# A quarter of the expert rows of the later prompt columns added by GpSimd to a sum of its own

## What is computed

```python
g = jax.nn.softmax(cv, axis=-1)
act = jax.nn.gelu(jnp.einsum('td,thkd->thk', xb, peer_u[e]).astype(jnp.float32))
return jnp.einsum('thk,thkd->td', (g * act).astype(xb.dtype), peer_v[e])
...
return x1 + peer_ffn(h, w_peer_q, peer_sub_keys, peer_u, peer_v).reshape(x1.shape)
```

## Time and profile before

| | |
|---|---|
| runs | 2168.15, 2169.51, 2175.05 us; median 2169.51 |
| profiled execution | 2170.43 us, of which the span (first to last instruction) 2168.6 |
| busy: PE, PEld | 1698.0 us (78%), 1236.0 us (57%) |
| busy: DVE, ACT, POOL | 1602.5 us (74%), 1257.1 us (58%), 635.5 us (29%) |
| HBM read | 690.14 MB |
| granted TensorE clock, mean | 0.835 |

### The profile page before, as it was taken

The page is one execution under the profiler, slowest core; times in us unless marked ns, Lnnn a source line. Parts: engine busy times, 40 slices in busy tenths (PEclk is TensorE's granted clock), DMA queues, the critical chain, the costliest instruction groups (busy, mean ns, idle before and its releaser), DMA issues.

```text
span 2168.6 us, 27262 instructions
## 1 busy us (share of the span) xinstructions
PE 1698.0 (78%) x8774; PEld 1236.0 (57%) x8774; DVE 1602.5 (74%) x3603; ACT 1257.1 (58%) x2751; POOL 635.5 (29%) x657
## 2 busy tenths in 40 slices
PE   7997699776896985996977987975887796765766
PEld 3554565635664654674655765654655665564554
DVE  2455676486699899869896796886898889768444
ACT  1223434226467654667897697874555465446665
POOL 1000000034334344333333333333333433333431
PEclk9998589886898886997998997987896897876666
DMA  7000300179999999999999999996999999999997
GB/s 277 20 17 13 88 1 30 49 284 420 417 414 390 419 418 390 419 379 384 419 419 374 406 400 371 419 411 248 412 368 362 405 370 385 316 417 358 420 420 302
DMA packets 108351, 695.68 MB, mean 321 GB/s; under 512 B 16688, under 2 KB 19120, under 8 KB 31408
## 3 DMA queue, kind: packets, MB, share of 16 engines
q0 software_dynamic: 95376, 674.29, 77.3%
q1 hardware_dynamic: 12832, 19.65, 3.0%
HBM read 690.14 MB, written 3.76 MB: 320 GB/s over the span
## 4 chain that ended last, share of the span: by engine, by line
PE 33%; DVE 30%; DMA 13%; ACT 10%; DVEq 4%; issue 4%; ACTq 3%; POOL 1%; POOLq 0%
DMA region<-in_peer_rows,region 12%; DVE region L1707 11%; DVE xall L1715 6%; PE ps L2244 5%; PE ps L2049 5%; DVEq L1112 4%; ACTq L1096 3%; ACT region L1100 3%; PE ps L1731 3%; PE ps L1996 2%; PE ps L2066 2%; ACT region L1097 1%; DVE region L1443 1%; PE ps L1899 1%; ACT region L1019 1%
## 5 line engine op out<-in xcount | busy, mean ns | idle before, releaser
L693 POOL DMA_INDIRECT region<-in_peer_rows,region x576 | 569.5, 989 | 1404.1 <-PE ps L2244 712.3
L1707 DVE SCALAR_TENSOR_TENSOR region<-region,h_now 128x1024 f32<-128x1024 f32 x576 | 695.7, 1216 | 208.5 <-DMA region<-in_peer_rows,region 191.8
L2244 PE MATMUL ps<-ident,region 128*128 128x128 f32 x3352 | 567.6, 327 | 253.9 <-ACT region L1100 231.8
L2244 PEld LDWEIGHTS ps<-ident,region 128*128 128x128 f32 x3352 | 472.6, 170 | 358.9 <-ACT region L1100 303.0
L1100 ACT ACTIVATE region<-region 128x1024 f32<-128x1024 f32 x419 | 481.3, 1149 | 35.5 <-issue 1.6
L1095 ACT ACTIVATE region<-region 128x1 f32<-128x1 f32 x576 | 114.5, 199 | 353.1 <-DVE region L1707 348.6
L2049 PE MATMUL ps<-w_uk_s,region 128*128 128x512 f32 x544 | 279.8, 640 | 7.1 <-ACT region L960 6.9
L1715 DVE SCALAR_TENSOR_TENSOR xall<-region,xall 128x1024 f32<-128x1024 f32 x157 | 201.8, 1285 | 68.3 <-ACT region L1097 53.3
L1097 ACT ACTIVATE region<-region 128x1 f32<-128x1 f32 x576 | 169.8, 295 | 40.7 <-issue 1.4
L2049 PEld LDWEIGHTS ps<-w_uk_s,region 128*128 128x128 f32 x544 | 100.2, 205 | 82.6 <-issue 73.9
L960 ACT ACTIVATE region<-ps 128x512 f32<-128x512 f32 x136 | 79.5, 585 | 68.7 <-PE ps L2049 66.0
(11 more groups left out here) (393 smaller groups left out, 2577.3 us busy)
## 6 DMA issues: line engine op xcount, KB each, us to landing
region<-in_w_peer_q POOLq DMA_DIRECT2D x16, 1024.0 KB
region<-in_peer_rows,region POOLq DMA_INDIRECT x576
region<-in_w_in POOLq DMA_DIRECT2D x8, 882.0 KB, 14.1
region<-in_w_peer_q SPq DMA_DIRECT2D x8, 512.0 KB, 4.3
region<-in_x_turned SPq DMA_DIRECT2D x5, 512.0 KB, 3.6
region<-in_w_out SPq DMA_DIRECT2D x2, 1024.0 KB, 12.4
region<-in_w_out SPq DMA_DIRECT2D x1, 2048.0 KB, 18.3
out_p_y<-xall SPq DMA_DIRECT2D x4, 512.0 KB
```

The lines of the kernel that those rows point to most:

```text
L693: pool.indirect_dma_start(ring[r][:], None, a["peer_rows"], bass.IndirectOffsetOnAxis(ap=experts[:, t, n:n + 1], axis=0)).then_inc(landed[ ...
L1707: v.scalar_tensor_tensor(ring[r][:, 0:D], ring[r][:, 0:D], 1.0, h_now[:], ALU.mult, ALU.mult, accum_out=acts[:, t % 2, n:n + 1]).then_inc( ...
L2244: last = te.matmul(ps[6 + c // 4][:, (c % 4) * P:(c % 4 + 1) * P], ring[r][:, D + c * P:D + (c + 1) * P], ident[:], is_transpose=True, sta ...
```

## The change

78 rows of the prompt, those with m >= 176, m % 128 >= 12 and m % 4 = 3, get a third way. ScalarE scales them as it does TensorE's (L1100). GpSimd then adds the scaled slot to `pool_acc`, which is `xall[:, 0, :]`, 128 x 1024 in f32, free once tile 0's y is stored. In GpSimd's queue the add stands just ahead of whatever is fetched into the same slot. VectorE adds `pool_acc` to `xall[:, t, :]` once a tile: at column 262 for tile 1, 390 for tile 2, and in `y_add(3)`; after the first two it clears `pool_acc` again, and the first time at column 174, after a wait for the store of y of tile 0. TensorE's `y_turn(1)` gets a wait for `sel_kept` of 2. `pool_rows`, `dve_rows` and `on_pe` replace the counts that assumed two ways.

Of the 78 rows, 63 were TensorE's and 15 VectorE's: 367, 375, 379, 399, 407, 415, 419, 427, 435, 439, 447, 455, 459, 467, 475.

```diff
--- before.py
+++ after.py
@@ -180,6 +180,7 @@
         HBUF_SLOT = len(ring)
         ring.append(Region(HBUF_AT, SIZE).view(W))
         NRING = len(ring)
+        pool_acc = xall[:, 0, :]
         h_rows = [hbuf] + [tables[:, 0:D]] * (NTILE - 1)
         late = Region(KEPT_END, OT_AT)
         I_ROW_AT = late.at
@@ -298,7 +299,7 @@
             "sk_in", "sk_turned", "skT_ready", "w_out_in", "g_ffn_in", "w_q0_in0", "w_q0_in1", "w_q0_in2", "w_used",
             "scored", "biased", "exped", "p_turned", "pT_ready", "attended", "normed_o", "o_turned", "oT_ready", "o_up", "mixed",
             "h_row", "h_turned", "h2T", "q_kept", "routed", "s_kept", "f_centered", "f_exped", "chosen",
-            "dotted", "v_scaled", "v_added", "v_mixed", "wts", "accT", "accT_s", "y_turned", "y_added", "y_out",
+            "dotted", "v_scaled", "v_added", "v_mixed", "v_pooled", "acc_ready", "wts", "accT", "accT_s", "y_turned", "y_added", "y_out",
             "made", "page_idx", "b_in", "b_new", "a_new", "pe_sq", "c_turned", "c_ready", "nope", "squared", "reduced", 
             "b_mean", "b_root", "bm_part", "bm_turned", "bm_diag", "bm_all", "b_centered", "b_exped", "b_sum", "b_weighted", "bo_scaled", "bo_turned", "bo_kept",
             "kidx_in0", "kidx_in1", "i_turned", "i_ready", "i_scored", "i_evac", "i_summed", "i_rows", "i_kept", "trial", "counted", "i_chosen", "i_back", "sel_kept",
@@ -346,7 +347,19 @@
 
 
 
+        POOL_FROM, POOL_EVERY = 176, 4
+
+        def on_pool(m):
+
+            return POOL_FROM <= m < SEQ and m % P >= 12 and m % POOL_EVERY == 3
+
+        def pool_rows(m):
+
+            return sum(on_pool(x) for x in range(m))
+
         def on_dve(m):
+            if on_pool(m):
+                return False
             if P <= m < SEQ and m % P < HEAD:
                 return True
             k = m + ADD_LAG
@@ -355,13 +368,20 @@
                     return m < SEQ and m * part % whole < part
             return False
 
+        def on_pe(m):
+            return not on_dve(m) and not on_pool(m)
+
         def pe_rows(m):
 
-            return sum(not on_dve(x) for x in range(m))
+            return sum(on_pe(x) for x in range(m))
+
+        def dve_rows(m):
+
+            return sum(on_dve(x) for x in range(m))
 
         def pe_ends(t):
 
-            own = [x for x in range(P * t, P * t + COLS[t]) if not on_dve(x)]
+            own = [x for x in range(P * t, P * t + COLS[t]) if on_pe(x)]
             return own[0], own[-1]
 
 
@@ -656,7 +676,20 @@
                         pool.wait_ge(S["made"], 4)
                     load_pages(v_s, a["cache_a_v"].rearrange("a (s j) h d -> (a s) (j h d)", j=PART), b, S["v_in"])
 
+            def add_row(m):
+
+                t, n = tile_of(m)
+                r = place_of["e", t, n]
+                pool.wait_ge(S["v_scaled"], m - dve_rows(m) + 1)
+                pool.wait_ge(S["acc_ready"], t)
+                hold(pool, S["v_pooled"], pool_rows(m))
+                nc.gpsimd.tensor_tensor(pool_acc, pool_acc, ring[r][:, D:W], ALU.add).then_inc(S["v_pooled"], 1)
+
             for f, what in enumerate(fetched):
+                if f >= NRING:
+                    kind, t, n = fetched[f - NRING]
+                    if kind == "e" and on_pool(P * t + n):
+                        add_row(P * t + n)
                 for batch in beside.get(f, ()):
                     load_batch(*batch)
                 kind, t, n = what
@@ -668,7 +701,9 @@
                     if kind_ != "e":
                         pool.wait_ge(S["w_used"], weights_used(fetched[f - NRING]))
                     elif on_dve(x):
-                        pool.wait_ge(S["v_mixed"], x - pe_rows(x) + 1)
+                        pool.wait_ge(S["v_mixed"], dve_rows(x) + 1)
+                    elif on_pool(x):
+                        pool.wait_ge(S["v_pooled"], pool_rows(x) + 1)
                     else:
                         pool.wait_ge(S["v_added"], pe_rows(x) + 1)
                 elif f == HBUF_SLOT:
@@ -1673,8 +1708,19 @@
                     v.tensor_tensor(x1, x1, ps[bank][:], ALU.add).then_inc(S["mixed"], 1)
                 yield
 
+            def add_pooled(t):
+                dve.wait_ge(S["v_pooled"], pool_rows(P * (t + 1)))
+                settle()
+                v.tensor_tensor(xall[:, t, :], xall[:, t, :], pool_acc, ALU.add)
+                settle()
+
+            def clear_pooled():
+                v.memset(pool_acc, 0.0).then_inc(S["acc_ready"], 1)
+
             def y_add(t):
                 yield
+                if t == 3:
+                    add_pooled(t)
                 dve.wait_ge(S["y_turned"], t + 1)
                 settle()
                 for j, bank in enumerate((3, 5)):
@@ -1696,6 +1742,12 @@
             for k in range(STEPS):
                 if k == MIXED_AT:
                     mix_rest()
+                if k == POOL_FROM - 2:
+                    dve.wait_ge(S["y_out"], 16)
+                    clear_pooled()
+                if k in (2 * P + 6, 3 * P + 6):
+                    add_pooled(k // P - 1)
+                    clear_pooled()
                 if k < NCOLS:
                     t, n = tile_of(k)
                     r = place_of["e", t, n]
@@ -2213,6 +2265,7 @@
                     pe.wait_ge(S["i_kept"], 5)
                 if t == 1:
                     pe.wait_ge(S["s_kept"], 4 * 4)
+                    pe.wait_ge(S["sel_kept"], 2)
                 if t == 2:
                     pe.wait_ge(S["ao_kept"], NB - 2)
                 for c in range(KD):
@@ -2230,7 +2283,7 @@
 
             for k in range(STEPS):
                 m = k - PE_LAG
-                if 0 <= m < NCOLS and not on_dve(m):
+                if 0 <= m < NCOLS and on_pe(m):
                     t, n = tile_of(m)
                     first, final = pe_ends(t)
                     if m == first:
@@ -2239,7 +2292,7 @@
                         else:
                             pe.wait_ge(S["mixed"], 8)
                     r = place_of["e", t, n]
-                    pe.wait_ge(S["v_scaled"], pe_rows(m) + 1)
+                    pe.wait_ge(S["v_scaled"], m - dve_rows(m) + 1)
                     for c in range(KD):
                         last = te.matmul(ps[6 + c // 4][:, (c % 4) * P:(c % 4 + 1) * P], ring[r][:, D + c * P:D + (c + 1) * P], ident[:], is_transpose=True,
                                          start=(m == first and c % 4 == 0), stop=(m == final), skip_group_check=True)
```

## The result

The changed kernel takes 2190.29 us (median of 4 runs, 2188.27 to 2192.80), the kernel before 2170.05 beside it: ratio 1.009, 95% interval [1.007, 1.011]. It is 20 us slower. The forecast was 2161, with a range from 2146 to 2180. Its profiled execution has a span of 2187.8 us.

The account below looks back on a forecast made before the run. DMA gathers were taken to bound most of the second part, VectorE columns 384 to 479. There -21.5 + 2.5 + 11.9 = -7.1 us, plus -1.5 us in columns 176 to 350, gave -8.6: 2161 us, range 2146 to 2180.

Parts of the forecast that it names:

- The lock: Columns 384 to 479: GpSimd's adds hold up VectorE's instructions with two SBUF inputs, 8.5 of 46 L1715, +11.9 us.
- The step that failed: Columns 176 to 350: DMA share 0.99 read as good as full, so the stretch stays unchanged within 2 us.
- VectorE's relief: Columns 384 to 479: twelve rows less on VectorE, 1.80 us each, take 21.5 us off VectorE.
- rival (a): Columns 384 to 479: lock eats the gain or ScalarE's 13.8 us return as wait; 2169 us, chance 0.27 with another rival.
- TensorE's relief: Columns 176 to 350: forty of 63 transposing bursts leave where the DMA is nearly full; taken as -1.5 us.
- The add: GpSimd's add of one 128x1024 row: between 1.285 and 2.80 us, taken as 2.80 us.
- The sums: VectorE adding and clearing GpSimd's sum: +2.5 us at column 390, nothing at 262 or in the last y.
- The waits: VectorE's wait at column 174 for the store of y and TensorE's before `y_turn(1)`: both cost nothing.
- Rival (b): Columns 384 to 479: every second add holds an L1715 for its whole length; slower, 2180 us, chance 0.21.

## Why the prediction was wrong

The forecast move without its lock, -21.5 + 2.5 - 1.5 = -20.5 us, was measured as -15.5, which is 5 us off. The lock was forecast at +11.9 us and measured at about +35, 23 us off. That is where the prediction fails.

- *The lock* was named, and its price in columns 384 to 479, +11.9 us, is near what was measured there: 12.2. L1767's mean of 1518 ns over 46 rows in the stretch gives (1518 - 1285) x 46 = 10.7 us of it. Some of the agreement is luck. Nine rows were held where 8.5 were forecast, though the adds took 2.376 us and not 2.80; with 2.376 the prediction's own sum is 7.2 x 1.19 = 8.6 us. (Its remark that an add of 2.25 us makes the price a fifth smaller is wrong by the same sum: the length of the add counts twice, and the price would be a third smaller, 7.7 us.) L1767 in the stretch in the changed kernel:

```profile
L1767 DVE SCALAR_TENSOR_TENSOR xall<-region,xall 128x1024 f32<-128x1024 f32 x46 | 69.8, 1518 | 27.5 <-ACT region L1132 24.3
```

- *The step that failed* is the one that read a DMA share of 0.99 in columns 176 to 350 as "as good as full" and so gave 40 adds there no price. It had the stretch "unchanged within 2 us". It became 9 to 16 us longer, and the adds there cost 17 to 21 us. The windows had the warning beside the share: 399 GB/s, where the best slices move 419 or 420. That is 5% of 498 us, by my estimate at most 25 us that the DMA could still give. The run without an add took part of it (407 GB/s, share 1.00), the change lost more (392). With VectorE busy 400.93 of 498.40 us and ScalarE 405.33, neither engine had much room; which of them bound the stretch, and where, isn't shown. Nor did I list VectorE's other instructions with two SBUF inputs. Of L1715 there are 15 in the stretch, but the routing, the mixer and the search have others: of the 25.1 us of stretching the 31 xors carry 13.3, though freeing them alone didn't lower the time.
- *VectorE's relief*, -21.5 us, was mis-sized. Without any add, columns 384 to 479 shorten by 7.6 us (317.0 to 309.4), and VectorE's rows alone give 4 us at the end. VectorE is busy 13.1 us less in the stretch (268.81 to 255.67: twelve rows, and the sum at 390 on top), and the idle time before L1767 stayed: 28.6 us in the run without an add, 29.6 before. So 12 x 0.51 us of idle time didn't go with the rows. This may be the part of rival (a) that has ScalarE's scalings come back as wait: ScalarE is busy 11.1 us more in the stretch (174.96 to 186.10), and the idle time per row of L1767 rose from 0.51 to 0.62 us. No run takes the two apart. L1767 in the stretch in the run without an add:

```profile
L1767 DVE SCALAR_TENSOR_TENSOR xall<-region,xall 128x1024 f32<-128x1024 f32 x46 | 59.1, 1285 | 28.6 <-ACT region L1132 25.3
```

- *TensorE's relief*, -1.5 us, was too small, for the same reason as the step that failed: TensorE's rows alone, without an add, are worth 4.1 us at the end. In columns 176 to 350 four traces with these rows moved and no reading instruction on GpSimd took 486.4 to 489.1 us, against 492.0 to 498.4 with the rows in place.
- *The add*: 2.376 us, within the bounds and below the 2.80 taken. (The estimate of 2.25 us from the figures of the Trainium skill, "GPSIMD Engine Reference", section 3.1, was nearer.)
- *The sums*: +2.5 us forecast for columns 384 to 479, nothing measured at the end. (In that stretch the trace of the sums alone is 3.7 us longer, 320.7 to 317.0.) The clearing took 912 ns. *The waits* at 174 and before `y_turn(1)` cost nothing that the run with the sums alone shows, as forecast.
- *Rival (b)*, the lock with 2180, had the sign, but the wrong place: it put the whole price into columns 384 to 479, by holds in step at every second add, where nine holds of 1.19 us were found for 21 adds. In the sum that the runs give, -15.5 + 34.8 = +19.3 us, the lock is the largest term, and two thirds of it lie elsewhere.

## What to carry to other kernels

An add on GpSimd isn't free time: price it by every VectorE instruction with two SBUF inputs in the whole stretch where it runs, not only by those of the line that is relieved, and move to GpSimd only rows that relieve VectorE itself. Call a stretch DMA-bound only if its GB/s, and not only its busy share, are those of the best stretch; at 0.99 and 95% of the rate, most of 25 us of another engine's time still got through. Price a relief by the fall in busy time, and not by the idle time before the line as well: here the idle time stayed when a fifth of the rows went.

## What the runs showed of the hardware

- A GpSimd f32 add of 128x1024 took 2.376 us in the mean, of 128x512 1.28, of 128x256 0.78; a clearing of 128x2048 1.82 and of 128x640 0.65; a multiplication of 128x2048 by a constant, in place, 5.39.
- Who was first can't be read from the recorded starts. In the two pairs of rows above, VectorE's instruction is recorded 0.28 and 0.48 us ahead of the add and was held all the same. But an unhindered xor takes 152 ns and would have been over before the add's recorded start. So the add held already before its recorded start, or the xor hadn't begun at its own. And in one pair VectorE, recorded 0.25 us ahead, kept its 1.22 us, and the add took 3.18:

```profile
1110.27 1.22 DVE L1385 TENSOR_TENSOR region<-region 128x2048 bf16<-128x2048 bf16 x1
...
1110.52 3.18 POOL L686 TENSOR_TENSOR xall<-xall,region 128x1024 f32<-128x1024 f32 x1 [0.82 <-ACT region L1135]
```

  (The Trainium skill, "SBUF — State Buffer", section "Who interferes with whom", has the first to issue hold the port pair that the two share, for the whole instruction. That VectorE with two SBUF inputs and a reading GpSimd instruction shut each other out agrees with these rows; who comes first can't be tested on them, and the next point but one bears on "whole".)
- A VectorE instruction with one SBUF tensor and a scalar read through a pointer wasn't held: 204 to 207 ns over 31, ten of them beside an add.
- The hold doesn't always last to the end of the GpSimd instruction. Beside an add the held xors ended within 0.03 us of its end. Beside the multiplication of 5.39 us the twelve held xors all ended 1.71 us before its end, and the held rows of L1767, which have 1.09 us still to run when they are let go, 0.64 us before it, for instance:

```profile
1267.02 5.41 POOL L686 TENSOR_SCALAR region<-region 128x2048 f32<-128x2048 f32 x1
1269.90 1.88 DVE L1767 SCALAR_TENSOR_TENSOR xall<-region,xall 128x1024 f32<-128x1024 f32 x1 [2.87 <-ACT region L1132]
```

- A GpSimd instruction that only writes left VectorE nearly alone: 1590.8 and 1591.2 us busy against 1588.9. (The Trainium skill, "SBUF — State Buffer", section "Who interferes with whom", has it so.)
- TensorE's granted clock in columns 176 to 350 was 0.89 before and 0.83 in the changed kernel, with 0.82 to 0.85 in the experiments in which 40 of its bursts were gone and the stretch took 486 to 504 us. 40 bursts of 1.09 us are 43.6 us, and TensorE's busy time fell by 25.5 us, so part of the relief was given back.
